# Modulation chunks and attention masks on VectorE, in a two-block kernel on one Trainium2 core

## The reference, cut to what matters

```
# first block: two branches, merged by gates
h     = rms_norm(x);  proj = h @ w_in
gates = sigmoid(proj[gate columns] + b_gate)
# stick-breaking attention, 8 heads of 64, queries in blocks of 128
strict   = key < query
log_fail = where(strict, log_sigmoid(-z), 0)
after    = reverse_cumsum(log_fail) - log_fail
w        = where(strict, exp(log_sigmoid(z) + after), 0);  o = w @ v
# RWKV7 time mixing: a recurrence with a 64x64 state per head, chunks of 64
x = x + rms_norm((gates * (both branches)) @ w_o);  x = x + rms_norm(swiglu(x))
# second block
mod = silu(c) @ w_ada + b_ada            # one row of 6144, from w_ada 1024 x 6144
sh1, sc1, g1, sh2, sc2, g2 = split(mod, 6)
h = rms_norm(x) * (1 + sc1) + sh1        # pooling and Mamba-2 mixers follow
x = x + g1 * (mixed @ w_out)
x = x + g2 * moe(rms_norm(x) * (1 + sc2) + sh2)   # 32 experts, in groups
```

## Time and profile before

| | |
|---|---|
| median of three runs | 1127.79 us (1127.28 to 1128.29) |
| the profiled execution's own time | 1126.72 us |
| its span, first to last record | 1124.6 us |
| mean granted TensorE clock | 0.992 of full speed |
| TensorE busy, matmul / weight load | 94% / 64% |
| VectorE, ScalarE, GpSimd busy | 41%, 32%, 4% |
| HBM | 316 MB, mean 281 GB/s |

### The profile page before, as it was taken

The page is one execution under the profiler, slowest core; times in us unless marked ns, Lnnn a source line. Parts: engine busy times, 40 slices in busy tenths (PEclk is TensorE's granted clock), DMA queues, the critical chain, the costliest instruction groups (busy, mean ns, idle before and its releaser), DMA issues.

```text
span 1124.6 us, 17911 instructions
## 1 busy us (share of the span) xinstructions
PE 1053.0 (94%) x7545; PEld 717.5 (64%) x7545; DVE 461.9 (41%) x698; ACT 354.3 (32%) x508; POOL 39.6 (4%) x32
## 2 busy tenths in 40 slices
PE   5999999999999999999999999999899989898986
PEld 5996777899699999877986453444244333242432
DVE  4784244467554453556657351222122212121212
ACT  5752322454463443355543220111011111010102
POOL 0002200002001010000000000000000000000000
PEclk9999999999999999999989999999999999999999
DMA  9454378335726556454366869999999999999994
GB/s 327 153 204 159 109 243 256 108 150 177 230 88 218 156 182 224 169 205 163 133 225 240 337 278 422 421 421 422 422 421 422 422 422 422 422 422 422 422 422 191
DMA packets 95445, 316.36 MB, mean 281 GB/s; under 512 B 8262, under 2 KB 33174, under 8 KB 70678
## 3 DMA queue, kind: packets, MB, share of 16 engines
q1 hardware_dynamic: 94342, 312.75, 72.4%
q10 hardware_dynamic: 1040, 2.69, 0.7%
HBM read 314.37 MB, written 1.05 MB: 280 GB/s over the span
## 4 chain that ended last, share of the span: by engine, by line
PE 72%; DMA 21%; DVE 4%; ACT 2%; issue 1%; SPq 0%; POOL 0%; DVEq 0%; ACTq 0%
DMA arena<-in_w 20%; PE bank L1480 12%; PE bank L769 11%; PE bank L771 11%; PE bank L770 11%; PE bank L1504 4%; PE bank L755 4%; PE bank L1027 3%; PE bank L942 2%; PE bank L1460 1%; PE bank L976 1%; PE bank L746 1%; PE bank L1517 1%; PE bank L716 1%; PE bank L728 1%
## 5 line engine op out<-in xcount | busy, mean ns | idle before, releaser
L1480 PE MATMUL bank<-ring,hT 128*64 128x512 f32 x512 | 226.6, 594 | 28.6 <-DMA arena<-in_w 27.5
L1480 PE MATMUL bank<-arena,hT 128*64 128x512 f32 x512 | 226.7, 595 | 0.0
L771 PE MATMUL bank<-h_high,ring_low 128*128 128x256 f32 x688 | 192.8, 280 | 0.0
L1480 PEld LDWEIGHTS bank<-ring,hT 128*64 128x64 f32 x512 | 67.9, 137 | 180.4 <-issue 130.7
L560 DVE TENSOR_TENSOR ring_low<-ring,hi_high 128x2048 fp32r<-128x2048 f32 (+2 forms) x58 | 126.0, 2218 | 100.8 <-ACT hi_high L1651 100.7
L769 PE MATMUL bank<-h_high,hi_high 128*128 128x256 f32 x528 | 147.8, 280 | 0.0
L770 PE MATMUL bank<-h_low,hi_high 128*128 128x256 f32 x528 | 147.2, 279 | 0.0
L1651 ACT ACTIVATE hi_high<-ring 128x2048 fp32r<-128x2048 f32 (+2 forms) x58 | 104.5, 1852 | 91.3 <-DMA ring<-in_w_ffn_up 33.5
L771 PEld LDWEIGHTS bank<-h_high,ring_low 128*128 128x128 f32 x688 | 129.9, 189 | 0.0
L1504 PE MATMUL bank<-arena 128*64 128x512 f32 x384 | 113.3, 595 | 7.1 <-DVE hT L2778 6.6
L2784 DVE TENSOR_TENSOR arena<-arena,bank 128x512 f32<-128x512 f32 x16 | 17.3, 1083 | 229.2 <-ACT arena L2008 229.2
(11 more groups left out here) (399 smaller groups left out, 1702.4 us busy)
## 6 DMA issues: line engine op xcount, KB each, us to landing
arena<-in_w SPq DMA_DIRECT2D x112, 1024.0 KB, 22.7
ring<-in_w SPq DMA_DIRECT2D x80, 1024.0 KB, 20.3
ring<-in_w_in SPq DMA_DIRECT2D x12, 2048.0 KB, 7.8
ring<-in_w_ada SPq DMA_DIRECT2D x7, 2048.0 KB, 8.2
ring<-in_w_ffn_gate SPq DMA_DIRECT2D x11, 1024.0 KB, 5.4
ring<-in_w_ffn_up SPq DMA_DIRECT2D x11, 1024.0 KB, 7.9
ring<-in_w_ada SPq DMA_DIRECT2D x20, 512.0 KB, 5.2
ring<-in_w_ffn_down SPq DMA_DIRECT2D x5, 2048.0 KB, 7.9
```

Source lines behind the costliest of these rows:

```text
L771: return mm(ps, a[1], b[0], start=False, stop=stop)
L1480: last = mm(both(6 + half, x), hg[:, k, (2 * q + x) * CAP:(2 * q + x + 1) * CAP], w13s[x][k // 4][:, k % 4, half * EF:(half + 1) * EF], st ...
```

## The change

It does five things.
1. Chunks 0 to 5 leave TensorE. VectorE makes their partial rows itself from the slot in SBUF: one product of 128x512 with a column of silu(c), and seven multiply-and-adds (`ada_products`). Chunks 0 to 3 stand among VectorE's attention work, 4 and 5 in the levels, two operations per level (the last six behind them). The slot is given free by `ada_acc`. TensorE keeps the sums, with ones instead of 1/32 (`cb` is scaled by 1/32 for chunks that stay); the sums of 0 to 2 move in between the score groups, 3 ahead of the third pair of heads, 4 to level 5, 5 behind "u".
2. Chunk 10 goes behind "u", chunk 11 behind the second "phi", and their sums behind the head means.
3. The attention additions and masks of GpSimd go to VectorE, and so does the making of `cb`.
4. ScalarE evicts gates 0 ahead of the exponential of the first half.
5. In the output projection the second tile's transposes stand between the first tile's halves, and chunk 9 behind them. The ring's slots are numbered so that the gate weights ("gate", 0) hold theirs while six loads take turns in the other two, and the paces are new.

```diff
-    for mm in range(2):
-        o += [("ga", mm)] + [("l", h) for h in range(4 * mm, 4 * mm + 4)]
+    o += [("ga", 0), ("l", 0), ("l", 1), ("as", 0), ("l", 2), ("l", 3)]
+    o += [("ga", 1), ("as", 1), ("l", 4), ("l", 5), ("as", 2), ("l", 6), ("l", 7)]
     o += [("tok", 1, a) for a in range(4)]
-    o += [("o", 0), ("o", 1)] + ada_banks(0) + [("o", 2), ("o", 3)]
+    o += [("o", 0), ("o", 1), ("as", 3), ("o", 2), ("o", 3)]
     both = [(i, q) for i in range(NT) for q in range(2)]
-    o += [("g", i, q, e) for i, q in both for e in range(2)] + ada_banks(1)
+    o += [("g", i, q, e) for i, q in both for e in range(2)]
     o += [("n", i, q) for i, q in both]
...
+        o += [("x", i, lv, q) for i, q in both] + ([("as", 4)] if lv == LEVELS - 1 else [])
         for i, q in both:
...
-    o += [("w1", i, q) for i, q in both] + ada_banks(LEVELS + 1)
-    o += [("u", i, q) for i, q in both] + ada_banks(LEVELS + 2)
+    o += [("w1", i, q) for i, q in both]
+    o += [("u", i, q) for i, q in both] + [("ad", 10), ("as", 5)]
     o += [("ry", 0, c) for c in range(2)] + [("psi", 0), ("psi", 1), ("phi", 1)]
-    o += [("ry", 1, c) for c in range(2)] + [("psi", 2), ("phi", 2)]
+    o += [("ry", 1, c) for c in range(2)] + [("psi", 2), ("phi", 2), ("ad", 11)]
     o += [("y", 0, 0), ("y", 0, 1), ("s", 1), ("y", 1, 0), ("y", 1, 1), ("s", 2)]
...
-    o += [("m", mm) for mm in range(2)]
+    o += [("m", mm) for mm in range(2)] + [("as", 10), ("as", 11)]
...
-ADA_EARLY = (0, 1, 2, 3, 4, 5, 10, 11)
+ADA_DVE = (0, 1, 2, 3, 4, 5)
...
         gate_columns(0)
         def modulation(c):
-            stream(("ada", c), [(0, cols(A["w_ada_2"][0], c * 512, c * 512 + 512))], ("ad", c))
-
-        for c in ADA_EARLY:
+            used = ("sem", "ada_acc", ADA_DVE.index(c) + 1) if c in ADA_DVE else ("ad", c)
+            stream(("ada", c), [(0, cols(A["w_ada_2"][0], c * 512, c * 512 + 512))], used)
...
-        PACED = {("ada", ADA_EARLY[3]): (("g", 0, 0, 0), ("g", 0, 1, 0), ("g", 1, 0, 0)),
-                 ("ada", ADA_EARLY[4]): (("n", 0, 0), ("n", 1, 0), ("x", 0, 1, 0)),
-                 ("ada", ADA_EARLY[5]): level_paces(1), ("ada", ADA_EARLY[6]): level_paces(2),
-                 ("ada", ADA_EARLY[7]): level_paces(3), ("gate", 1): level_paces(4), ("gate", 2): level_paces(5),
-                 ("gate", 3): (("u", 0, 0), ("u", 0, 1), ("u", 1, 0))}
+        held = [key for key, _, _ in W].index(("gate", 0))
+
+        def slot_of(n):
+
+            if n <= held:
+                return n % RING
+            if n <= held + 6:
+                return (held + 1 + (n - held - 1) % 2) % RING
+            return (n - 1) % RING
+
+        last_level = LEVELS - 1
+        PACED = {("ada", 11): (("dt", 0, last_level - 1, 1), ("dt", 1, last_level - 1, 1), ("x", 1, last_level, 0)),
+                 ("gate", 1): (("w1", 1, 0), ("u", 0, 0), ("u", 1, 0)),
+                 ("gate", 2): (("phi", 1), ("ry", 1, 0), ("phi", 2)),
+                 ("gate", 3): (("y", 0, 1), ("y", 1, 0), ("y", 1, 1))}
...
-            loads[n % RING] += 16 * (4 if key in PACED else len(parts))
-            SLOTS[key] = (n % RING, loads[n % RING])
+            loads[slot_of(n)] += 16 * (4 if key in PACED else len(parts))
+            SLOTS[key] = (slot_of(n), loads[slot_of(n)])
...
-                drained(pe, ("ad", c))
+                if c in ADA_DVE:
+                    pe.wait_ge(S("ada_acc"), ADA_DVE.index(c) + 1)
+                else:
+                    drained(pe, ("ad", c))
...
                     for k in range(KD):
-                        last = mm(ps[o:o + 64, k:k + 1], modp[c][:, 64 * k:64 * k + 64], K("thirty_second")[:, 0:1],
+                        last = mm(ps[o:o + 64, k:k + 1], modp[c][:, 64 * k:64 * k + 64], K("ones")[:, 0:1],
...
                 else:
-                    last = mm(ps[:, 0:512], K("thirty_second"), modp[c], start=True, stop=True)
+                    last = mm(ps[:, 0:512], K("ones"), modp[c], start=True, stop=True)
...
-            def ada(turn):
-
-                if turn:
-                    ada_sum(ADA_EARLY[turn - 1])
-                if turn < len(ADA_EARLY):
-                    ada_chunk(ADA_EARLY[turn])
...
+                    if h:
+                        ada_sum(h // 2 - 1)
                     pe.wait_ge(S("att_sp"), j + 1)
...
-                    ada(0)
+                    ada_sum(3)
...
                 grams(i, q)
-            ada(1)
...
-                ada(lv + 1)
+                if lv == LEVELS - 1:
+                    ada_sum(4)
...
-            ada(LEVELS + 1)
...
-            ada(LEVELS + 2)
+            ada_chunk(10)
+            ada_sum(5)
...
+            ada_chunk(11)
...
+            ada_sum(10)
+            ada_sum(11)
...
+            mix_transposes(0)
+            ada_sum(8)
+            drained(pe, ("pm",))
+            mixed_out(0, 0)
+            mix_transposes(1)
+            mixed_out(0, 1)
+            ada_chunk(9)
+            mixed_out(1, 0)
+            ada_sum(9)
+            mixed_out(1, 1)
...
             to_tokens(0)
+            gates_of(0)
             weights(0)
-            gates_of(0)
...
             for p in range(PAIRS):
-                if p == 2:
-                    ada_rows(0)
...
-            ada_rows(ADA_EARLY[1])
...
-                ada_rows(ADA_EARLY[lv + 1])
...
-            ada_rows(ADA_EARLY[LEVELS + 1])
...
+            ada_rows(10)
+            ada_rows(11)
...
-            pool.wait_ge(S("csil"), 1)
-            nc.gpsimd.tensor_copy(cb, csil.unsqueeze(2).to_broadcast([P, KD, 32])).then_inc(S("cb"), 1)
-            strict = K("strict").unsqueeze(1).unsqueeze(1).to_broadcast([P, 4, 2, P])
-
-            def diagonal(buf, half):
-
-                return buf[:, 4 * half:4 * half + 4, :].rearrange("p h (b t) -> p h b t", b=3)[:, :, 0:3:2, :]
-
             pool.wait_ge(S("con_in"), 16)
-            for half in range(2):
-                pool.wait_ge(S("att_ln"), half + 1)
-                hs = slice(4 * half, 4 * half + 4)
-                nc.gpsimd.tensor_tensor(rz[:, hs, :], rz[:, hs, :], az[:, hs, :], ALU.add).then_inc(S("att_sum"), 1)
-                pool.wait_ge(S("att_sum"), half + 1)
-                nc.gpsimd.tensor_tensor(diagonal(rz, half), diagonal(rz, half), strict, ALU.mult).then_inc(S("att_sp"), 1)
-            for half in range(2):
-                pool.wait_ge(S("att_x"), half + 1)
-                nc.gpsimd.tensor_tensor(diagonal(az, half), diagonal(az, half), strict, ALU.mult).then_inc(S("att_w"), 1)
...
+            strict = cast(K("strict").unsqueeze(1).unsqueeze(1), P, 4, 2, P)
+
+            def diagonal(buf, half):
+
+                return buf[:, 4 * half:4 * half + 4, :].rearrange("p h (b t) -> p h b t", b=3)[:, :, 0:3:2, :]
+
+            def one_minus(half):
+
+                dve.wait_ge(S("att_ln"), half + 1)
+                hs = slice(4 * half, 4 * half + 4)
+                link(V.tensor_tensor(rz[:, hs, :], rz[:, hs, :], az[:, hs, :], ALU.add))
+                V.tensor_tensor(diagonal(rz, half), diagonal(rz, half), strict, ALU.mult).then_inc(S("att_sp"), 1)
+
+            def weights(half):
+
+                dve.wait_ge(S("att_x"), half + 1)
+                V.tensor_tensor(diagonal(az, half), diagonal(az, half), strict, ALU.mult).then_inc(S("att_w"), 1)
+
+            def ada_products(c, k0, k1):
+
+                w, acc = slot_view(("ada", c), KD), modp[c]
+                if k0 == 0:
+                    arrived(dve, ("ada", c))
+                    dve.wait_ge(S("csil"), 1)
+                for k in range(k0, k1):
+                    if k == 0:
+                        ins = V.tensor_scalar(acc, w[:, k, :], csil[:, k:k + 1], None, ALU.mult)
+                    else:
+                        ins = V.scalar_tensor_tensor(acc, w[:, k, :], csil[:, k:k + 1], acc, ALU.mult, ALU.add)
+                    if k < KD - 1:
+                        link(ins)
+                    else:
+                        ins.then_inc(S("ada_acc"), 1)
...
+                if i == 0:
+                    ada_products(0, 0, 5)
+                one_minus(i)
...
+            def later_weights(h):
+                for e in range(2):
+                    ps = filled(dve, ("l", h + e))
+                    V.tensor_scalar(az[:, h + e, :], ps[:, 0:384], 0.0, None, ALU.min).then_inc(*free(("l", h + e)))
+
...
+            ada_products(0, 5, KD)
+            to_tokens(0)
+            ada_products(1, 0, KD)
+            later_weights(0)
+            ada_sum(0)
+            ada_products(2, 0, KD)
+            later_weights(2)
+            ada_sum(1)
+            ada_products(3, 0, 4)
+            weights(0)
+            later_weights(4)
+            ada_products(3, 4, KD)
+            ada_sum(2)
+            later_weights(6)
+            to_tokens(1)
+            weights(1)
+            ada_sum(3)
+            V.tensor_scalar(cb, cast(csil.unsqueeze(2), P, KD, 32), 1.0 / 32, None, ALU.mult).then_inc(S("cb"), 1)
             dve.wait_ge(S("gate_in"), 48)
...
```

(13 more changed lines are left out.)

51 lines of the change are left out of this document (16 added, 35 removed).

## The result

| | kernel before | the change |
|---|---|---|
| median of 20 runs | 1128.62 us (1127.28 to 1132.67) | 1133.21 us (1128.13 to 1136.88) |
| ratio | | 1.0029, 95% interval 1.0017 to 1.0041 |
| the profiled execution | 1126.72 us, span 1124.6 | 1136.19 us, span 1133.8 |
| mean granted clock of it | 0.992 | 0.984 |

The kernel became 0.3% slower, some 3.3 us by the ratio (4.6 between the two medians), where 7.1 us of gain was forecast.

A forecast was written before the change was run, and what follows sets the result against it. TensorE was taken as the bound where the change acts, VectorE mostly waiting. Attention +4.7, levels -17.2 and +1.4, work behind them +4.0 gave -7.1 us: 1119.6 from 1126.72 profiled, 1120.7 as median; range 1116.0 to 1126.5.

The forecast's parts named there:

- the levels: WKV levels, grams to "ry": six chunks and six sums leaving give -17.2 us, uncovered evictions of the grams +1.4.
- DMA. ... Nothing waits: Loads of gate columns 1 to 3: issued from some 187 us, in time for TensorE at 209; no cost.
- The clock, a rival with a chance of 0.13: Wait before third pair of heads: TensorE's clock falls, costing 1.4 to 3.7 us, 1122 to 1124.5; chance 0.13.
- a sum of -4 to -6: Whole kernel: the change's total in us if, by the Trainium skill's rule, the clock falls in the new wait.
- There at 131.7: Attention stage: chunk 3's load, issued at 123.6 us behind seven small loads, has landed at 131.7.
- the rival that the chunks were cover for the round trip by ScalarE and VectorE: WKV levels: the round trip overruns 0.45 us of slack, five levels wait up to 1 us: +5, 1125.7; chance 0.10.
- The product step: VectorE's two-input operation of 128x512 on a chunk: 0.69 us, 0.72 with the gap; near ends 0.66 and 0.75.
- dear VectorE: VectorE's operations beside loads cost 1.083 us instead of 0.69, factor 1.57: +16.5 us, 1137.2; chance 0.10.
- The prices of the masks: Attention stage on VectorE: addition of 128x1536 takes 1.76 us, a mask of 1024 takes 1.23.
- The output projection: Moving the second tile's transposes between the first tile's halves keeps TensorE's work and ends: nothing gained or lost.
- ScalarE's order: Attention stage: gates 0 first costs one table load (1.28 us) inside 13.41 us of idle time; nothing on the path.
- What stands behind 216 us moves as a block: Everything after 216 us, expert stream included, shifts together, since the sync queue waits for a sum of the scan.

The follow-up runs named there:

- Later paces: The change with the loads of gate weights 2 and 3 paced later, off the state products; 1128.18 us, ratio 0.9996 to the kernel before.
- the filled wait: The change with 5 and 4 useless matmuls of 128x256 in TensorE's two waits of the attention stage; 1126.19 us, ratio 0.9976 to the kernel before.
- small-loads kernel: The change with the seven small loads behind chunk 5 in the sync queue instead of ahead of chunk 3; 1130.62 us, ratio 1.0016 to the kernel before.
- the last version: The change with later gate weights, small loads before branch weights, chunk 10 loaded before 5, chunk 3's last steps and sum later; 1120.26 us, ratio 0.9923.
- work in the wait, long: The change with 11 and 10 useless matmuls of 128x256 in TensorE's two waits of the attention stage; 1131.19 us, ratio 1.0015 to the kernel before.

## Why the prediction was wrong

**The sum.** Forecast were 209.2 us for the gate columns (216.3 less 7.1), measured 220.8: 11.6 us, in four stretches.

| | forecast | measured | gap |
|---|---|---|---|
| third pair of heads | 144.8 | 147.1 | +2.3 |
| from there to the grams | 1.5 | 2.8 | +1.3 |
| grams to "ry" | 45.6 | 46.9 | +1.3 |
| "ry" to gate columns | 17.3 | 24.0 | +6.7 |

By cause, 2.3 us are the late third pair, 3.1 the longer waits for instructions behind "ry", and the other 6.2 nearly all the lower clock behind both.

**"DMA. ... Nothing waits" is the step that failed**: it leads to the largest gap, the +6.7, with 3.1 us of waiting and the fall of the clock behind it. It asked whether a load comes in time for its user, and they did. It didn't ask what a load does to TensorE's instructions. The gate weights, which before came in from 183 us on beside the levels, now go out from 193.65, all three in 20.7 us, onto the state products. The DMA share there was 0.57 from 203 to 208 us and 0.01 from 208 to 212.5; now it is 1.04 and 0.95 (200 to 210). TensorE had 0.51 us of "issue" there before; now 0.86 + 2.74. Later paces took 5.0 us back, and a stream put beside the levels made two such waits where none had been. The trace of before had a sign of it, 1.14 us in level 1 beside a DMA share of 0.92 (154 to 156 us):
```profile
157.95 3.89 PE L1027 MATMUL bank<-arena 64*64 64x64 f32 x126 [1.14 <-issue]
```
In its later levels no such wait follows though the stream goes on (a share of 0.70 and more from 162 to 203 us). There a sum and a chunk, 2.8 us in few matmuls (162.82 to 165.66), stood in every level, and the change took them out. That they covered the fetching of instructions fits these rows, but no run tests it alone. The Trainium skill (Runtime: NRT & Kernel Launch, Instruction fetch mechanics) says that instructions come in blocks of 16 KiB over a DMA queue of the engine's own, and calls the cost mostly hidden. The size agrees with the page of the profile; that it is hidden doesn't hold here, with waits up to 3.58 us beside a full stream.

**The clock, a rival with a chance of 0.13, came true twice.** Once at the waits of 2.18 and 1.62 us, and once at the one of 2.74. The wait was forecast as one of 3.6 us ahead of the third pair; it came as 3.8 in two parts, the first because the second pair's bank hung on sum 2. Its price was put at 1.4 to 3.7 us; the first fall cost 1.3 + 1.3 here (0.35 of it an "issue" wait in the grams), and 2.2 by the filled wait. Of the +6.7 behind "ry", 3.1 are the longer "issue" waits; 1.8 are the head means (3.75 us instead of 1.96), 0.5 the two sums behind them (2.59 instead of 2.1), and the other 1.3 lie in the state products, with a clock of 0.50 from 210 to 215 us. I had weighed the case down with a single row, 0.87 us of idleness without a fall, though the wait I forecast myself was four times as long. The Trainium skill's rule (TensorE: Matmul & The Clock Gate, Part 1: The HAM clock gate), by which I called this case the likelier one, was the better guide, and the chance should have followed. My estimate by it, a sum of -4 to -6, was off too, as it knew nothing of the late instructions.

**Chunk 3.** Its issue was right to 0.3 us (123.6 and 123.87). "There at 131.7" was 2.2 us early: 8.1 us is the time of chunk 1's load; here the data began later and chunk 4's load was beside it. From its landing to the end of the last mask I had 13.1 us, and 13.2 were measured.

**Right:** the levels. But for the grams (5.0 us instead of 3.65) the stage took what the forecast said, six chunks and six sums less, with VectorE busy for 34.6 us of 46.9; the rival that the chunks were cover for the round trip by ScalarE and VectorE is false. The product step was 0.77 us (seven in 5.4, start to start), 0.05 over the value taken and 0.02 over the near end, far from 1.08: dear VectorE is false as well. The prices of the masks (1.76, 1.23) came out to a hundredth. The output projection and ScalarE's order cost nothing, as said. "What stands behind 216 us moves as a block" held up to the first feed-forward load (+4.46 us, 283.27 against 278.81). From there the profile of the change falls back further, to +9.2 at the end of the span: 1.8 us with the slower feed-forward rate, 1.6 in the first expert loads with the falls of the clock there (58.1 us instead of 56.5), the rest in the expert loop. The medians of 20 runs differ by 4.6, so what comes on top of the 4.5 belongs mostly to these two executions.

**What stays open:** why the instructions of the filled-wait kernel come in time behind the last sum, where the same stream makes them late in the change; what sets the rate of a feed-forward step; and where the small-loads kernel loses 4 us behind its gate columns.

## What to carry to other kernels
When work leaves TensorE for another engine, list what its new waits do to the clock, and fill or remove each; waits of 2.18 and 1.62 us cost another 2.2 to 2.6 behind them. When loads move, look at what runs beside them, and keep a full stream away from stretches of short matmuls, where TensorE uses up its instructions fastest. The offload can pay: the last version keeps it, with the late chunk and the stream out of the way, and is 8.7 us under the kernel before. What the same moves of loads give without the offload wasn't run.

## What the runs showed of the hardware
- TensorE's instructions arrive in 16 KB pieces, five in 22 us of quiet levels, some 125 matmuls of 64x64 each. Beside a stream TensorE waited for them up to 3.58 us (work in the wait, long), and each wait of 0.8 us or more ended 1.2 to 1.5 us behind a piece's landing.
- Matmuls without a use kept the granted clock at 1.00 through two waits in which it fell to half otherwise. A wait of 2.15 us in the last version, with nothing in it, came without a fall; in the one of 2.31 us of the small-loads kernel the clock fell, and there the one-column matmuls of sum 3 (1.05 us) stood ahead of it. The length alone doesn't say which.
- VectorE's product steps were slowed beside GpSimd's additions and masks: 7.34 us for three instead of 2.32, and 1.38 instead of 0.48 for the one with one input.
- A feed-forward step takes 11.31 or 11.52 us at a granted clock of 1.00 (323 to 420 us), constant within an execution, both seen in the same kernel and on each of three chips.
